# MoE token rows gathered and expert results returned by one-hot matmuls on TensorE instead of through a row table in DRAM

## The reference

```python
def swiglu(h, w13, w2):
    gate, up = jnp.split(h @ w13, 2, axis=-1)
    return (jax.nn.silu(gate) * up) @ w2

def moe_swiglu(h, router, w13, w2):
    logits = (h @ router).astype(F32)
    top_val, top_idx = lax.top_k(logits, TOP_K)
    weights = jax.nn.softmax(top_val, axis=-1)
    combine = jnp.einsum('blk,blke->ble', weights,
                         jax.nn.one_hot(top_idx, N_EXPERTS, dtype=F32)).astype(h.dtype)
    out = jnp.zeros_like(h)
    for e in range(N_EXPERTS):
        out = out + combine[..., e:e + 1] * swiglu(h, w13[e], w2[e])
    return out
```

## Time and profile before

| | us |
|---|---|
| median of 3 runs (lowest, highest) | 2268.61 (2264.15, 2269.34) |
| profiled execution, its own time | 2267.49 |
| its span in the trace | 2265.4 |

### The profile page before, as it was taken

The page is one execution under the profiler, slowest core; times in us unless marked ns, Lnnn a source line. Parts: engine busy times, 40 slices in busy tenths (PEclk is TensorE's granted clock), DMA queues, the critical chain, the costliest instruction groups (busy, mean ns, idle before and its releaser), DMA issues.

```text
span 2265.4 us, 55614 instructions
## 1 busy us (share of the span) xinstructions
PE 2119.4 (94%) x24430; PEld 1563.7 (69%) x24430; DVE 1154.6 (51%) x1544; ACT 920.5 (41%) x1208; POOL 195.5 (9%) x200
## 2 busy tenths in 40 slices
PE   8999999999999999999999889997999799979986
PEld 4677567788888657888888768844883488348832
DVE  2544695422233396666666448802870287038602
ACT  4422023422222284555555247702760376037500
POOL 2000471100000022000000120000000000000000
PEclk9999999999999999999999999999999999999998
DMA  8566307233332421222220379999999999999995
GB/s 290 196 224 230 112 1 226 90 93 94 94 104 98 135 87 60 63 62 62 62 63 25 97 297 354 358 392 403 406 405 406 405 406 398 406 403 406 401 390 237
DMA packets 229011, 512.14 MB, mean 226 GB/s; under 512 B 15367, under 2 KB 108447, under 8 KB 228511
## 3 DMA queue, kind: packets, MB, share of 16 engines
q1 hardware_dynamic: 226238, 499.22, 59.6%
q10 hardware_dynamic: 1442, 6.06, 0.8%
q0 software_dynamic: 1152, 4.19, 0.6%
HBM read 492.67 MB, written 16.78 MB: 225 GB/s over the span
## 4 chain that ended last, share of the span: by engine, by line
PE 74%; SPq 9%; DMA 7%; DVE 4%; ACT 3%; issue 2%; POOL 0%; ACTq 0%; DVEq 0%
PE bank L1795 14%; SPq L930 8%; PE bank L1825 7%; DMA expert_w<-in_moe_w_dram 4%; PE bank L1267 4%; PE bank L1268 4%; PE bank L1269 4%; PE bank L1879 3%; PE bank L1173 2%; PE bank L1144 2%; PE bank L1399 2%; PE bank L1145 2%; PE bank L1146 2%; PE bank L1435 2%; PE bank L1285 2%
## 5 line engine op out<-in xcount | busy, mean ns | idle before, releaser
L3300 DVE TENSOR_TENSOR w_low<-expert_w,w_high 128x1792 fp32r<-128x1792 f32 (+1 forms) x192 | 385.8, 2024 | 126.5 <-ACT w_high L2430 125.5
L2430 ACT CAST w_high<-expert_w 128x1792 fp32r<-128x1792 f32 (+1 forms) x192 | 324.9, 1699 | 112.6 <-PE bank L1795 79.8
L1879 PE MATMUL bank<-expert_w,arena 128*64 128x448 f32 x1024 | 204.1, 551 | 28.9 <-DMA expert_w<-in_moe_w_dram 28.5
L1795 PE MATMUL bank<-w_high,xg_high 128*128 128x448 f32 x512 | 152.3, 379 | 30.7 <-DVE xg_low L3290 30.7
L1879 PEld LDWEIGHTS bank<-expert_w,arena 128*64 128x64 f32 x1024 | 76.6, 139 | 146.9 <-issue 145.8
L1795 PE MATMUL bank<-w_low,xg_high 128*128 128x448 f32 x512 | 150.1, 375 | 0.0
L1795 PE MATMUL bank<-w_high,xg_low 128*128 128x448 f32 x512 | 149.6, 374 | 0.0
L1267 PE MATMUL bank<-u_high,ring_high 128*128 128x512 f32 x352 | 139.1, 395 | 1.7 <-DVE u_low L2946 1.7
L1268 PE MATMUL bank<-u_low,ring_high 128*128 128x512 f32 x352 | 139.1, 395 | 0.0
L1269 PE MATMUL bank<-u_high,ring_low 128*128 128x512 f32 x352 | 138.6, 394 | 0.0
L3397 DVE TENSOR_TENSOR arena<-arena,bank 128x448 f32<-128x448 f32 x16 | 9.9, 621 | 238.3 <-PE bank L1879 238.3
(11 more groups left out here) (474 smaller groups left out, 4122.1 us busy)
## 6 DMA issues: line engine op xcount, KB each, us to landing
expert_w<-in_moe_w_dram SPq DMA_DIRECT2D x128, 1792.0 KB, 20.7
expert_w<-in_moe_w_dram SPq DMA_DIRECT2D x32, 2048.0 KB, 21.6
arena<-in_mod_w_dram SPq DMA_DIRECT2D x48, 1024.0 KB, 8.7
expert_w<-in_moe_w_dram SPq DMA_DIRECT2D x32, 1536.0 KB, 20.8
arena<-in_ffn_w_dram SPq DMA_DIRECT2D x44, 512.0 KB, 5.1
arena<-in_hy_w_in_dram SPq DMA_DIRECT2D x12, 1024.0 KB, 5.3
arena<-in_rw_w_rkv_dram SPq DMA_DIRECT2D x48, 256.0 KB, 2.9
arena<-in_ffn_w_dram SPq DMA_DIRECT2D x11, 1024.0 KB, 4.9
```

Of the source, the lines that this page charges most:

```text
L1795: last = pe.matmul(bank[b0 + v][:, 0:EH], x[:, k, :], w_[:, kk, v * EH:v * EH + EH], start=(k == 0 and x is XGH and w_ is wh), stop=(k == ...
L1879: last = pe.matmul(b[hd(v), 0:EH], small_x[:, k, :], w[:, kk, v * EH:v * EH + EH], start=(k == 0), stop=(k == KT - 1))
L2430: act.copy(high_piece(kind, n), piece(kind, ering[q % ERN], n // 2, n % 2))\
L3300: dve.tensor_tensor(piece(kind, low[s], n // 2, n % 2), piece(kind, ering[s], n // 2, n % 2), high_piece(kind, n).bitcast(F32), ALU.subtract)\
```

## The change

The row table in DRAM is gone, with its clearing, the indirect transfers, `fetch_rows` and the writes of yields. In its place:

- `gather` on PE makes the next expert's slots out of `UTOK` (all tokens, which now stay in SBUF) and `pick`: 16 fp32 matmuls, over 64 columns ahead of a small expert and over 128 ahead of a large one.
- DVE scales each yield with the slot's share and the gate row (`yield_small`, `yield_large`); PE multiplies it with `pickT` (`combine`, 4 fp32 matmuls of 512 columns); DVE adds the four banks to `XTOK` (`added`), which ACT has scaled by ALPHA.
- The yield and the combine of a small expert stand at the head of the next `large` (in the first couple on zero shares), those of a large expert within the `small` of the same couple, behind its first gate products.
- Each engine reads the pass count at the end of a pass. The shares are made by POOL, and their first three steps stand earlier in DVE's routing chain.
- The end needs no table rows: `small_rows` of the last expert is combined as before.

```diff
-            def turn_rows(b0, item):
-                pe.wait_ge(sem("rows_back"), 16 * (2 * N_EXP + 2) + 16 * item + 16)
-                settle(pe)
-                for k in range(KT):
-                    last = pe.transpose(bank[b0 + k // 4][:, (k % 4) * P:(k % 4) * P + P],
-                                        gathered_rows[:, k * P:(k + 1) * P], ident)
+            def gather(b0, n=P):
                 for k in range(KT):
                     for tt in range(2):
+                        last = pe.matmul(bank[b0 + k // 4][:, (k % 4) * P:(k % 4) * P + n],
+                                         UTOK[:, tt, k * P:(k + 1) * P], pick[:, tt, 0:n], start=(tt == 0), stop=(tt == 1))
+            def combine(banks, rows):
+                for tt in range(2):
+                    for half in range(2):
+                        last = pe.matmul(bank[banks[2 * tt + half]][:, :], *rows(tt, half), start=True, stop=True)
                 return last
...
@@ PE, large @@
                     if c == 0:
+                        step(pe, "expert_vectors", "small_yield", couple)
+                        settle(pe)
+                        combine((6, 7, 2, 3), of_small).then_inc(sem("expert_products"), 1)
                         step(pe, "expert_vectors", "xg_low", couple)
...
                     if c == 0:
-                        step(pe, "expert_vectors", f"small_h{EC - 1}", couple - 1)
+                        step(pe, "expert_vectors", "small_added", couple)
...
-                turn_rows(0, item).then_inc(sem("expert_products"), 1)
+                gather(0, SMALL).then_inc(sem("expert_products"), 1)
...
@@ PE, small @@
+                    if c == 1:
+                        step(pe, "expert_vectors", "large_added", couple)
                     small_products("gate", c, couple)
...
+                    else:
+                        step(pe, "expert_vectors", "large_yield", couple)
+                        settle(pe)
+                        combine((6, 7, 1, 3), of_large).then_inc(sem("expert_products"), 1)
                     small_products("up", c, couple)
...
-                turn_rows(0, item).then_inc(sem("expert_products"), 1)
+                gather(0).then_inc(sem("expert_products"), 1)
...
@@ DVE @@
+            def added(banks):
+                for tt in range(2):
+                    for half in range(2):
+                        o = XTOK[:, tt, half * 512:half * 512 + 512]
+                        last = dve.tensor_tensor(o, o, bank[banks[2 * tt + half]][:, :], ALU.add)
+                last.then_inc(sem("expert_vectors"), 1)
+            def yield_small():
+                for half in range(2):
+                    last = dve.scalar_tensor_tensor(out=small_rows[hd(half), :], in0=bank[4][hd(half), :],
+                                                    scalar=slot_share[hd(half), 0:1],
+                                                    in1=rowG[hd(half), half * 512:half * 512 + 512],
+                                                    op0=ALU.mult, op1=ALU.mult)
...
+            passes_made = dve.value_load(passes[0:1, 0:1], min_val=1, max_val=2)
+            step(dve, "expert_products", f"small_down{EC - 1}_1", passes_made * PAIRS - 1)
+            step(dve, "expert_vectors", f"small_h{EC - 1}", passes_made * PAIRS - 1)
+            yield_small().then_inc(sem("last_yield"), 2)
             dve.wait_ge(sem("ld_last_rows"), 32)
-            dve.wait_ge(sem("rows_moved"), 128)
-            for tt in range(2):
-                o = OUT[:, tt, :]
-                link(dve.tensor_tensor(o, o, rowG, ALU.mult))
-                dve.scalar_tensor_tensor(out=o, in0=XTOK[:, tt, :], scalar=float(ALPHA), in1=o, op0=ALU.mult,
-                                         op1=ALU.add).then_inc(sem("rows_scaled"), 1)
-            link(dve.tensor_scalar(rowG, rowG, slot_share[:, 0:1], None, ALU.mult))
```

More of the change, by code:

```diff
@@ L2667, in _ @@
+            row_step(last)
+            row_step(pool.tensor_tensor(comb, comb, by_second, ALU.add))
+            for q in range(2):
+                last = pool.tensor_copy(shares[:, :, q * N_EXP:(q + 1) * N_EXP], comb)
+            last.then_inc(sem("routed"), 1)
         @block.vector
@@ L3214, in _ @@
             ahead_unit(0)
-            link(dve.memset(nothing, 0.0))
+            step(dve, "ahead_vectors", "key_unit", 0)
             for d in range(2):
@@ L3235, in _ @@
             dve.memset(slots, -1.0)
+            dve.memset(pickT, 0.0)
             link(dve.memset(shares, 0.0))
@@ new lines, in yield_small, with yield_large @@
+            def yield_small():
[4 more added lines that the diff above has]
+                                                    op0=ALU.mult, op1=ALU.mult)
+                return last
+            def yield_large():
+                for half in range(2):
+                    cs = slice(half * 512, half * 512 + 512)
+                    last = dve.scalar_tensor_tensor(out=large_rows[:, cs], in0=bank[4 + half][:, :], scalar=slot_share[:, 0:1],
+                                                    in1=rowG[:, cs], op0=ALU.mult, op1=ALU.mult)
+                return last
@@ L3369, in large @@
                     low_digits("gate", c, couple, range(1, PIECES))
+                    if c == 0:
+                        step(dve, "expert_products", "small_combined", couple)
+                        step(dve, "expert_vectors", "xg_low", couple)
+                        added((6, 7, 2, 3))
                     if c == 1:
```

201 lines of the change are left out of this document (63 added, 138 removed).

## The result

| us | before | after |
|---|---|---|
| median (lowest, highest) | 2267.48 (2264.15, 2269.34), 4 runs | 2237.07 (2235.12, 2238.91), 4 runs |
| profiled execution, own time (span) | 2267.49 (2265.4) | 2238.85 (2237.1) |

The ratio is 0.9867 (0.985 to 0.9884): 30.4 us faster by the medians, 28.6 by the profiled executions. Predicted were 2250 and a range of 2240 to 2262, so the gain of 18.3 us was too small by 10 or 12, and the range missed the time. The median of before is that of four runs, one more than in the table ahead of the prediction.

A forecast was written before the change was run, and what follows sets the result against it. The prediction took transfers to bound couples 2 to 4, with PE close behind. It summed 5.5 (couples), 8.1 (fetches), 4.7 (tail) and 0 (couple 1 and start) to 18.3 us won, forecasting 2250 us, range 2240 to 2262.

The forecast's parts named there:

- table bytes less starvation, couples 2 to 4: Each couple saves 4.5 us of table transfers and loses 2.7 to transfers without a free buffer: 1.8 won, 5.5 in three.
- indirect fetches: POOL's indirect fetches in couple 4 go, winning 8.1 us, with 5.2 by their bytes as the lower bound.
- tail: After the last products, the statistics start sooner without DVE's work on table rows and gate: 4.7 us won.
- couple 1 and start: First products 2.5 us sooner (up to 4.8 with the clock), offset in couple 1 by gather, combine and stall: 0.
- clearing: Dropping the table's 512 KB writes from SP's queue in the RWKV stage wins 0, as no engine waits behind them.
- I take 2.7: Per couple, transfers finding no free buffer because PE is later lose 2.7 us, about the middle of the possible loss.
- a margin of nothing: At a large expert's end the DMA queue is barely full, so PE's 5.0 us lateness per couple can starve transfers.
- the prediction's 1.5 us: PE's full clock, if kept, gives back 1.5 us of the transfers' loss in a couple.
- the 0.9 for an earlier routing: At the start, the routing ends 0.9 us earlier, part of first products coming at 1351.6 instead of 1354.12.
- rival (c): DVE's additions and yield stall PE at each large expert's head, making the kernel slower: 2282; chance 0.05.
- rival (b): PE takes all: full starvation and DVE stall in each couple, only 3.6 to 11.3 us won; chance 0.18.
- Rival (a): Transfers never starve, two loads in flight suffice: 26 to 29 us won, 2240 to 2243; chance 0.17.

The follow-up runs named there:

- 2: Changed kernel with the row table's bytes put back as idle writes nobody waits for, 1.84 MB per couple; 2251.91 us.
- 6: Changed kernel loading three of four weight tiles for gate and up of the small experts, PE's instructions unchanged; 2221.54 us.
- 5: Changed kernel with the products that return a large expert's results (`combine`) made twice; 2245.21 us.
- 12: The changed kernel run once more, unchanged, for a second trace; 2234.71 us.
- 15: Kernel before, loading three of four weight tiles for gate and up of the small experts; 2211.92 us, one run.
- 3: Kernel before without POOL's last four indirect fetches, OUT cleared instead; 2262.9 us, ratio 0.9983.
- 11: Kernel before with the wait for the LayerNorm's rows moved behind the last yield; 2262.56 us, ratio 0.9975.
- 9: Changed kernel with the pass count read ahead of the loop again on PE, ACT and DVE; 2241.09 us.
- 1: Changed kernel with the table's clearing put back, 18 writes of 512 KB in SP's queue in the RWKV stage; 2242.7 us.
- 13: Changed kernel with the table's clearing put back and made twice, 36 writes of 512 KB; 2247.82 us.
- A: The changed kernel itself, against the kernel before; median 2237.07 us, ratio 0.9867.
- 14: Changed kernel with the products that return a large expert's results (`combine`) made four times; 2270.16 us, one run.
- 4: Changed kernel with the gather for the next large expert moved behind the small expert's last down products; 2249.66 us.
- 8: Changed kernel with the gather behind the small expert's last down products and PE's loop over the four couples written out; 2240.22 us.

## Why the prediction was wrong

| term, us won | predicted | measured, profiled executions | shown by |
|---|---|---|---|
| table bytes less starvation, couples 2 to 4 | 3 x 1.8 = 5.5 | 3.9, 3.5, and in couple 4 what the fetches leave of 13.3 | 2, 6, 5, 12, 15 |
| indirect fetches | 8.1 | 6.5 to 9.0 by traces, 1 to 7 by runs | 3, 11, 15 |
| tail | 4.7 | 5.4 | 11 |
| couple 1 and start | 0 | 0 | 9 |
| clearing | 0 | 2.1 | 1, 13 |

**The step that failed: "I take 2.7", the starvation.** The prediction took a couple as the transfers' time plus PE's new lateness as far as buffers do not cover it, and set that against "a margin of nothing". In each of couples 2 and 3 A won 3.7 us of the bytes' 4.5, so the new work took 0.8 back (1.4 in the second trace) and not 2.7. A couple goes nearly by the longer of two cycles, and the two were far apart. Experiments 6 and 15 measure PE's own cycle, at 214.4 us after and at most 208.3 before; the transfers' is 88.1 MB at 0.404 MB per us, 218.0, and 222.6 with the table's bytes. Side by side (5 and 14 with 3.7 and 11.1 us added to PE's cycle; the last column is what the couple takes over the longer of the two):

| kernel | PE | transfers | couple | over the longer |
|---|---|---|---|---|
| before (2, 3) | 208.3 | 222.6 | 223.4 | 0.8 |
| experiment 2 | 214.4 | 222.6 | 223.0 | 0.4 |
| after, two traces | 214.4 | 218.0 | 219.5 | 1.5 |
| experiment 5 | 218.1 | 218.0 | 221.0 | 2.9 |
| experiment 14 | 225.5 | 218.0 | 227.5 | 2.0 |

The starvation is real: in these rows of after, at the end of the large experts, stands what the earlier trace rows had, some of it deeper:

```profile
1690.00:1695.00 5.00, 5.00 (x24) 4.14 (x23) 0.00 (x0) 0.00 (x0) 0.00 (x0) 1.00 0.79 269
1695.00:1700.00 5.00, 5.00 (x27) 2.56 (x27) 1.41 (x2) 0.00 (x0) 0.00 (x0) 1.00 0.95 364
...
1910.00:1915.00 5.00, 5.00 (x24) 4.14 (x23) 0.00 (x0) 0.00 (x0) 0.00 (x0) 1.00 0.96 355
...
2130.00:2135.00 5.00, 5.00 (x24) 3.89 (x24) 0.00 (x0) 0.00 (x0) 0.00 (x0) 1.00 0.92 332
```

But the loss was there before (0.8), and it grew by 0.7 in the two traces of A and not at all in experiments 1, 9 and 13 (0.4 to 0.7 over the transfers), not by 2.7. With PE's cycle as long as the transfers' (experiment 5) it is 2.9, of which up to 1.6 may be the jump. That PE lies 7 us above and the loss is still 2.0 (experiment 14) says that two whole cycles are not the full account. As the rows read, PE is the slower one in the large experts, until the ring is full and the transfers sag, and in the small ones it catches up with them, even where its whole cycle is the longer. This is the mechanism that the prediction had; its size for this change was wrong.

**Why PE was not later at those places.** The prediction had PE 2.5 us later at the end of a large expert and the combine's 3.4 on top. The large expert with its pause is about as long as before, 131.5 to 133.2 us in the two traces of A against 132.4 to 133.0, though the gather costs 2.6 more: the pause shrank from 8.05 to 6.5. The pause ends a fixed chain after the weights land (table load 1.28, high digits 1.69, low digits 2.02, `xg_low` 1.29), and before PE stood ready 1.7 us ahead of the landing, now at it:

```profile
2003.24 1.28 ACT L2420 ACT_TABLE_LOAD   x1 [9.08 <-DMA expert_w<-in_moe_w_dram]
2004.54 1.69 ACT L2420 CAST w_high<-expert_w 128x1792 fp32r<-128x1792 f32 x1
...
2005.44 3.56 PE L1759 MATMUL bank<-arena 64*128 64x512 f32 x8 [2.24 <-DVE arena L3307]
...
2009.73 0.67 PE L1778 MATMUL bank<-w_high,xg_high 128*128 128x448 f32 x2 [0.72 <-DVE xg_low L3237]
```

The clock helped too, as the prediction's 1.5 us allowed: in the 10 us behind the pauses the clock granted was 0.70 to 0.76, and is 0.83 to 1.00 now. At the head of couple 3, before, then after:

```profile
1798.10:1808.10 10.00, 10.00 (x35) 9.01 (x36) 8.02 (x5) 6.44 (x5) 0.00 (x0) 0.70 1.03 403
1790.54:1800.54 10.00, 9.86 (x48) 8.92 (x48) 10.00 (x9) 7.55 (x6) 0.00 (x0) 1.00 1.03 404
```

In the small experts PE idled 8.5 us of 88.4 for weights; the combine and the gather lie there. The prediction used this idle time for PE's pace ("3.1 us a load against 4.54") and not as room.

**The clearing, "and no engine waits there for a transfer behind them: 0".** It cost 2.7 us on the average of the traces, and twice the writes cost 8. The 2.1 of the table are what is left here of 3.6 won in that stretch, since the way from there to the first expert weights took 1.5 us more; that way varies from 64.3 to 70.2 us between the traces. The prediction also read 50 to 98 GB/s for the stage, where the earlier trace rows show 60 to 63. That the writes cause PE's waits of the kind issue is shown by 13; how is not. The Trainium skill, "Runtime: NRT & Kernel Launch", section "Instruction fetch mechanics", has an engine's instructions come by DMA as well. Whether the writes delay those, no run here shows: from 850 to 1245 us the instruction packets of the larger queue are 68 or 69 and take 1.1 or 1.2% of the engines' time, in A and in experiments 1 and 13 alike, but when they were wanted is not recorded.

**The fetches** at 8.1 lie within the traces' 6.5 to 9.0 and above the runs' 1 to 7. The 13.3 us of couple 4 are that, the bytes' 3.6, and 1 to 3 us by which one execution's couple differs from another's.

**The tail** was right, with PE's read of the count at nothing rather than 1.1. **The start** was right in sum and too large in its part: the count is worth 1.6 us (9), and the 0.9 for an earlier routing did not come, since the router's products took 5.30 us (5.33 in the second trace) against 3.95. That the first products came at 1351.86, where 1351.6 was predicted, is luck: the mixture of experts had begun 2.1 us sooner. The slow router products are a matter of the clock: the clock granted from 1332 to 1337 is 0.66 on average, between the levels of 1.2 and 2.4 GHz, where before it stayed at 1.00 through them; PE had waited 2.1 us ahead of them both times. PE's timeline of after:

```profile
1332.11 5.30 PE L1715 MATMUL bank<-arena 128*8 128x256 f32 x16 [2.13 <-ACT arena L2379]
...
1343.11 3.81 PE L1751 MATMUL bank<-arena 128*128 128x128 f32 x32 [0.23 <-DVE arena L3232]
```

**Prices.** The 64-column gather takes 3.68 us (3.6 predicted by the row over 8 columns):

```profile
1463.58 3.68 PE L1751 MATMUL bank<-arena 128*128 128x64 f32 x32
```

The Trainium skill, "TensorE: Matmul & The Clock Gate", section "Back-to-back issue gap", gives a formula for isolated matmuls, by which it would be about half, and says that it does not give the pace of a stream. The trace bears that out for this stream of fp32 matmuls: 0.23 us apiece over 64 columns, 0.24 over 128. The large `combine` took 3.70 us (3.4 predicted). `added` took 2.47 us (2.8 predicted), and nothing stalled ahead of up, so rival (c) had no ground. PE's cycle in rival (b), 215.6 us, was 1.2 over the measured one; (b) drew from it that PE takes all, where 3 us under the transfers meant that it takes little. Rival (a), at a chance of 0.17, came nearest in time with 26 to 29 us won. But its ground, transfers that never starve, is not what the rows show (269 GB/s), couple 1 gave nothing where it had 2 us, and the clearing's part was not in it.

**Open:** how the writes of the clearing reach PE, what in experiment 5 is the products' and what the jump's, and why the medians of experiments 3 and 9 differ from those of their base by other amounts than the traces.

## What to carry to other kernels

Where an engine and the transfers share a ring, work out each one's own cycle in full, and compare the two before adding any lateness. Here idle time of the shorter one was room for nearly all the new work while 3.6 us (2%) of 218 were left between them; a loss of 2 to 3 us came when PE's cycle was as long as the transfers' or longer, probably because the ring of 8 limits how far one can run ahead within a cycle. Measure the cycle that is hidden by making the other cheaper (fewer bytes, the same instructions); one run shows it. Background writes that nobody waits for were not free here beside a stage that is full on PE: price them by a run with twice as many.

## What was not expected of the hardware

- A jump back in PE's loop cost 4.43 us from the end of a stream of short matmuls to the next instruction (experiments 4 and 8). In A, where PE waits 2.3 us for the yield at this place, nothing is seen of it; in experiment 5, at the same place with more code in the loop, the wait is 3.7 to 4.0 us of the kind issue, but in experiment 14, with more code still, it is the 2.3 us again.
- 18 writes of 512 KB, with 60 to 63 GB/s moved in all where 35 are moved without them, lengthen a stage in which PE is busy 97% by 2.7 us on average, 36 by 8, with waits of the kind issue and 0.2 and 0.7 us of waits for a transfer.
- The 17 traces, whose kernels hardly differ at their start, lie up to 7.6 us apart in their first 50 us (SP's load of `in_hy_w_in` is issued at 42.2 to 49.9 us); the two traces of A lie 0.1 apart. A difference of 2 us is to be read from the length of its stage.
